# First attention stage of a two-block transformer kernel: order of DVE's work at two tiles of a head pair, the rotation's PSUM read, and three matmuls at the opening

## What is computed

```
qa = _rms(aq.reshape(B, N, ATT_KV_HEADS, ATT_GROUP, ATT_HEAD_DIM), att_q_norm).transpose(0, 2, 3, 1, 4)
ka = _rms(ak.reshape(B, N, ATT_KV_HEADS, ATT_HEAD_DIM), att_k_norm).transpose(0, 2, 1, 3)
q_lat = _rope(qa[:, :, :, n_ctx:], cos, sin)
k_all = jnp.concatenate([ka[:, :, :n_ctx], _rope(ka[:, :, n_ctx:], cos, sin)], axis=2)

s = jnp.einsum('bhgqd,bhkd->bhgqk', q, k, preferred_element_type=jnp.float32) * (ATT_HEAD_DIM ** -0.5)
p = jax.nn.softmax(s, axis=-1).astype(v.dtype)
return jnp.einsum('bhgqk,bhkd->bhgqd', p, v)
```

## Time and profile before

| what | value |
|---|---|
| median of 3 runs | 4217.92 us (4216.91 to 4218.13) |
| the profiled execution's own time | 4220.12 us |
| its span in the trace | 4218.3 us |
| PE busy | 3938.0 us (93%) |
| DVE busy | 1680.2 us (40%) |
| ACT busy | 851.4 us (20%) |
| POOL busy | 692.3 us (16%) |
| this phase, 308 to 498 us | 190 us |

### The profile page before, as it was taken

One profiled execution on the slowest core, in us unless ns is written; L12 is line 12 of the kernel. 1 busy time (PEld: TensorE's weight loads), 2 busy tenths in 40 slices (PEclk: granted clock), 3 DMA queues, 4 the chain that ended last, 5 costly groups with the idle time before them and its releaser, 6 DMA issues. The chain is left out here.

```text
span 4218.3 us, 51374 instructions
## 1 busy us (share of the span) xinstructions
PE 3938.0 (93%) x20867; PEld 2405.2 (57%) x20867; DVE 1680.2 (40%) x3134; ACT 851.4 (20%) x1663; POOL 692.3 (16%) x513
## 2 busy tenths in 40 slices
PE   7998889999999999899998999989998898999988
PEld 4565445554448666488745677768654444443333
DVE  2337343323764554533474656634124324111111
ACT  3224320000121333200013333321113201000000
POOL 0003212222420111123342332310002200000000
PEclk9999999999999999899998999999989998999999
DMA  5107611112541100254352010014200314999999
GB/s 175 40 11 285 198 40 60 60 60 95 170 126 56 46 31 26 93 217 160 111 173 50 26 31 26 19 39 154 63 0 1 155 46 192 406 420 422 422 421 374
DMA packets 323233, 580.12 MB, mean 138 GB/s; under 512 B 58700, under 2 KB 189228, under 8 KB 322360
## 3 DMA queue, kind: packets, MB, share of 16 engines
q1 hardware_dynamic: 323000, 576.83, 37.3%
HBM read 566.15 MB, written 10.63 MB: 137 GB/s over the span
## 5 line engine op out<-in xcount | busy, mean ns | idle before, releaser
L3348 PE MATMUL dn_ps<-room,dn_w 128*128 128x512 f32 (+1 forms) x616 | 230.2, 520 | 0.5 <-DVE dn_v_tok L3897 0.3
L961 PE MATMUL ffn_up_ps<-ffn_up_t,room 128*128 128x384 f32 (+1 forms) x704 | 208.3, 440 | 8.0 <-DVE room L1037 8.0
L961 PE MATMUL ffn_up_ps<-room 128*128 128x384 f32 (+1 forms) x704 | 203.9, 433 | 0.0
L4907 PE MATMUL experts_ps<-experts_ring,experts_xs 128*64 128x512 f32 (+1 forms) x768 | 164.1, 580 | 21.9 <-DMA experts_ring<-in_w_up 21.9
L961 PEld LDWEIGHTS ffn_up_ps<-ffn_up_t,room 128*128 128x128 f32 x704 | 136.0, 194 | 66.1 <-DVE room L1037 9.5
L1233 PE MATMUL ffn_down_ps<-ffn_down_w_sums,ffn_w 128*128 128x512 f32 x330 | 163.1, 604 | 10.8 <-DVE ffn_down_w_sums L1321 10.8
L2637 PE MATMUL hgrn_ps<-room,hgrn_w 128*128 128x512 f32 x372 | 170.3, 593 | 0.9 <-DVE hgrn_v L2891 0.9
L4907 PE MATMUL experts_ps<-experts_ring,room 128*64 128x512 f32 (+1 forms) x768 | 161.1, 570 | 8.7 <-DMA experts_ring<-in_w_up 8.1
L961 PEld LDWEIGHTS ffn_up_ps<-room 128*128 128x128 f32 x704 | 134.0, 190 | 55.5
L1044 DVE TENSOR_TENSOR room<-ffn_up_ps,room 128x384 f32<-128x384 f32 (+1 forms) x154 | 73.4, 489 | 222.2 <-PE ffn_up_ps L961 222.2
L5001 DVE TENSOR_TENSOR x_sb<-x_sb,experts_ps 128x512 f32<-128x512 f32 x56 | 38.5, 688 | 297.9 <-PE experts_ps L4842 297.9
(11 more groups left out here) (682 smaller groups left out, 7315.3 us busy)
## 6 DMA issues: line engine op xcount, KB each, us to landing
experts_ring<-in_w_gate SPq DMA_DIRECT2D x128, 704.0 KB, 14.9
experts_ring<-in_w_up SPq DMA_DIRECT2D x128, 704.0 KB, 16.7
experts_ring<-in_w_down SPq DMA_DIRECT2D x160, 512.0 KB, 13.7
att_wm<-in_mod_w SPq DMA_DIRECT2D x20, 2048.0 KB, 8.9
ffn_w<-in_ffn_w_down SPq DMA_DIRECT2D x37, 1024.0 KB, 4.9
ffn_up_wm<-in_ada_w SPq DMA_DIRECT2D x12, 2048.0 KB, 12.6
ffn_w<-in_ffn_w_up SPq DMA_DIRECT2D x22, 1024.0 KB, 7.6
ffn_front<-in_ffn_w_down SPq DMA_DIRECT2D x18, 1024.0 KB, 4.8
```

Source lines behind the costliest of these rows:

```text
L961: mm = nc.tensor.matmul(result(n, p), lhs[:, k, :], rhs[:, k, :], start=k == 0, stop=k == half - 1)
L3348: mm = nc.tensor.matmul(out, ahead.tile[:, k, :] if k < by_ahead else wt[:, h % 2, piece, k, :], hT[:, k, tok], start=k == 0, stop=k == KD ...
L4907: mm = nc.tensor.matmul(ps[out_rows, 3 * n + c, 0:b - a], xs_now[:, j, at:at + SLOTS], ring[:, w_at + a:w_at + b], start=j == 0, stop=j == ...
```

## The change

It has three parts, all in `even_attention`.

1. **First tile.** In pairs 2, 3 and 4 DVE runs the reciprocal and the normalising of unit `u` ahead of `highest(u + 1)`. At all other tiles the order is as before.
2. **Rotation.** `rope` is split. `rope_by_sin`, which reads bank 7, stands at the end of DVE's third tile, with its wait for `swapped`. `rope_by_cos` and the sum stay in the fourth tile. PE's `turn(u, 1)` of the fourth tile waits for the sine product alone (`rotated`), and the second wait for `roped`, ahead of the modulation, is gone.
3. **Opening.** Ahead of its first wait in the phase PE issues three float32 matmuls of 128x512 from the identity matrix into bank 6. Nobody reads their result.

```
+def keep_busy(nc, out, lhs, rhs, n):
+    for _ in range(n):
+        nc.tensor.matmul(out, lhs, rhs, start=True, stop=True)
...
+            keep_busy(nc, ps[:, 6, :].rearrange("p (a n) -> p a n", a=4), ident, ident.unsqueeze(1).broadcast_to([P, 4, P]), 3)
             pe.wait_ge(S["two_set"], 4)
...
                 if at == 3 and j + 1 < PAIRS:
-                    pe.wait_ge(S["roped"], j + 3)
+                    pe.wait_ge(S["rotated"], 2 * (j + 2) + 1)
...
-                if at == 3 and j + 1 < PAIRS:
-                    pe.wait_ge(S["roped"], j + 3)
...
-            def rope(i, bank, n):
+            def rope_by_sin(bank, n):
                 dve.wait_ge(S["swapped"], n)
                 if n > 1:
                     dve.wait_ge(S["roped"], n - 1)
+                nc.vector.tensor_tensor(tmp[:, 0, :], ps[:, bank, :], sin[:, :], ALU.mult).then_inc(S["rotated"], 1)
+
+            def rope_by_cos(i, n):
                 lat = raw[:, i, CTX:]
-                nc.vector.tensor_tensor(tmp[:, 0, :], ps[:, bank, :], sin[:, :], ALU.mult).then_inc(S["rotated"], 1)
                 nc.vector.tensor_tensor(tmp[:, 1, :], lat, cos[:, :], ALU.mult).then_inc(S["rotated"], 1)
                 dve.wait_ge(S["rotated"], 2 * n)
                 nc.vector.tensor_tensor(lat, tmp[:, 0, :], tmp[:, 1, :], ALU.add).then_inc(S["roped"], 1)
...
+            for u, (j, t) in enumerate(units):
+                at = u % TILES
+                after_context = at == 0 and j
+                if after_context:
+                    normed_b(u)
+                if u + 1 < len(units):
+                    highest(u + 1)
+                if not after_context:
+                    normed_b(u)
                 if u == 0:
                     modulated(len(OPENING_BANKS), OTHER)
                 if j + 1 < PAIRS and at == 3:
                     dve.wait_ge(S["gained"], j + 2)
-                    rope(j + 1, OTHER, j + 3)
+                    rope_by_cos(j + 1, j + 3)
                 if u < TILES:
                     read_out(u)
                 if at - 1 in mod_at(j):
                     modulated(OPENING + LOOP * j + mod_at(j).index(at - 1), OTHER)
                 if j + 1 < PAIRS and at == 1:
                     gained(j + 1)
+                if j + 1 < PAIRS and at == 2:
+                    rope_by_sin(OTHER, j + 3)
```

More of the change, by code:

```diff
@@ L2367, in _ @@
             dve.wait_ge(S["gained"], 1)
-            rope(0, 4, 1)
+            rope_by_sin(4, 1)
+            rope_by_cos(0, 1)
             dve.wait_ge(S["k_scaled"], 2)
-            rope(KEY, 5, 2)
+            rope_by_sin(5, 2)
+            rope_by_cos(KEY, 2)
             for m, bank in enumerate(OPENING_BANKS):
@@ L2392, in highest, with normed_b @@
                     nc.vector.scalar_tensor_tensor(s[:, 1, a:a + 1], s[:, 0, a:a + 1], -1.0, rs[:, j, t, a:a + 1], ALU.mult, ALU.mult).then_inc(S["max_done"], 1)
-            highest(0)
-            for u, (j, t) in enumerate(units):
+            def normed_b(u):
+                j, t = units[u]
                 s = st[:, u % 2, :, :]
-                at = u % TILES
-                if u + 1 < len(units):
-                    highest(u + 1)
                 dve.wait_ge(S["exp_done"], 2 * u + 2)
@@ L2406, in _ @@
                 nc.vector.tensor_scalar(flat, flat, s[:, 3, 1:2], None, ALU.mult).then_inc(S["b_normed"], 1)
+            highest(0)
+            for u, (j, t) in enumerate(units):
[7 more added lines that the diff above has]
+                    normed_b(u)
                 if u == 0:
```

## The result

The changed kernel takes 4232.9 us in the median of 6 runs (4227.95 to 4236.88), the kernel before 4218.02 us (6 runs, 4215.26 to 4218.85). The ratio is 1.0036, with a 95% interval of 1.0023 to 1.0049: 15 us slower. The forecast was 6.7 us slower and its range ended at 4231.0. So the sign of the sum was right, its size was not.

A forecast was written before the change was run, and what follows sets the result against it. The prediction took PE, nearly always busy but with 35 us idle between its pieces, as the bound. First tiles -4.0, rotation waits +9.0, clock +2.2 and opening -0.5 gave +6.7 us, so 4224.6 us, range 4218.5 to 4231.0.

The forecast's parts named there:

- The term of 9.0 us for the waits: At three rotations, PE's second transposes start 3.0 us later each, behind DVE's late normalising and POOL's 3.15 us call.
- The first tiles: First tiles of pairs 2 to 4: earlier normalising gains 1.8, 1.8 and 0.4 us, 4.0 us in all.
- the clock term: PE's longer idle time at the rotations makes half clock likely: 2.2 us lost, between 0 and 4.6.
- The price of one spell: Half clock behind a rotation costs 0.8 us on the second transposes and up to 1.1 us on the modulation.
- The discount of half for cover: Much of the half-clock cost at a rotation lies over waits, so 1.1 us was taken, a little more than half.
- already pays for one: Pair 1's rotation has half clock in the kernel before, so the clock loss counts twice 1.1 us, not three times.
- The opening: Three matmuls ahead of PE's stream at the phase's start: 0.5 us gained, bounded by DVE's 0.60 us of idle time.
- The spreading half clock: Rival, chance 0.28: half clock covers transposes and modulation at all three rotations; +11.2 us, 4229.1 us.
- The rule of the Trainium skill: By it POOL would keep 2.63 us and block DVE's cosine product; the prediction held that the trace disagrees.
- POOL at 2.63 us: Rival, chance 0.14: POOL's call at the rotations is not stretched and the clock holds; +3.0 us, 4220.9 us.
- the late stream: Rival, chance 0.04: PE's opening stream ends late at half clock, 1.8 us lost; +9.0 us, 4226.9 us.
- the swap lands in time: Rival, chance 0.04: the swap precedes DVE's arrival, so each rotation saves PE's 1.19 us; -8.1 us, 4209.8 us.

The follow-up runs named there:

- second trace: The changed kernel run and traced again with no edit; 4231.2 us, ratio 1.003 to the kernel before.
- split alone: The changed kernel without the opening matmuls and with the first tiles in their old order, leaving only the rotation's split; 4235.23 us, ratio 1.0038 to the kernel before.
- part 3 alone: The kernel before plus only the three opening matmuls; 4219.87 us, ratio 1.0006.
- cosine early: The changed kernel with DVE's cosine product moved ahead of the swap in the third tile and the sum moved to the fifth tile; 4226.99 us, one run.

## Why the prediction failed, by its own steps

**What came as written.** At each rotation PE waits 2.58 us on DVE (2.7 predicted) and 1.30, 1.30 and 0.92 on POOL (1.4), DVE idles 2.61 us ahead of the sine product (2.6), and POOL takes 3.15. The term of 9.0 us for the waits measures 3 x 2.94 = 8.8. The first tiles in pairs 2 and 3 gave 1.8 and 2.1 us against 1.8 each, pair 4's 0.45 (456.01 to 462.57 before, 470.74 to 476.85 now) against 0.4: 4.3 against 4.0. For pairs 2 and 3 that agreement is partly luck. The forecast had 1.3 us for the new order and 0.5 for the clock, but of the gain about 1.3 and 1.6 us are half clock that went away with the 2.07 us gap; what the new order buys at full clock is pair 4's 0.45. The start at 384.60 from which the 1.3 us were counted was itself late by half clock: the scores ahead of it took 2.41 us, 1.56 at full clock.

**The step that failed is the size of the clock term.** The forecast said: a spell costs up to 0.8 us on the second transposes and up to 1.1 on the modulation, "much of it will lie over waits, so I take 1.1 us". The pieces above 22.65 us are 3.65, 2.55 and 3.46 in the changed kernel, 2.27, 3.36 and 2.36 in its second trace, and 2.61, 2.75 and 2.82 with the split alone: 2.9 us on average in nine rotations, and none without. Before paid 1.5 in pair 1 (21.23 - 19.71). The term is therefore 9.7 - 1.5 = 8.1 us in the profiled execution (2.1, 2.5 and 3.5 us in pairs 1 to 3, where 0, 1.1 and 1.1 stood), 6.5 in the second, where 2.2 stood and 4.6 was the upper bound. Two things were wrong in it:

- The price of one spell. I took the modulation from rows 10, 3.00 us, but that was one which the clock left on its way; one wholly at half clock takes 3.60, 1.67 above 1.93. And the spell reaches further than the two rows that I priced. Pair 1 shows it:

```profile
365.20 1.97 PE L2200 MATMUL att_ps<-cst,att_probs 128*128 128x128 f32 x8 [1.30 <-POOL att_probs L2324]
367.89 1.09 PE L2223 MATMUL att_ps<-cst,room 128*128 128x128 f32 x4 [0.72 <-ACT att_pT L2304]
...
372.43 1.12 PE L2200 MATMUL att_ps<-cst,att_probs 128*128 128x128 f32 x4
373.48 1.81 PE L2168 MATMUL att_ps<-even_raw 64*128 64x256 f32 x8
```

  Against the same rows at full clock (1.09, 0.63, 0.66 and 1.56 us) these are 0.88 + 0.46 + 0.46 + 0.25 us, with the modulation's 1.67 in all 3.72. The piece was 3.65 us longer.
- The discount of half for cover. 3.72 by the rows and 3.65 by the piece means that, from the second transposes on, next to nothing was covered; in pairs 2 and 3 the same sums give 2.61 and 3.52 us by the rows and 2.55 and 3.46 by the piece. The wait behind the second transposes, on ACT's copy, was 0.72 us and 0.77 before, so it hid 0.05. Only what is slowed ahead of the wait on POOL is covered: in pair 3 the scores took 1.08 us in place of 0.70, and that wait was 0.92 us in place of 1.30. Neither of the two rows that I priced stands there.

Pair 1 "already pays for one" was right in kind and too much in size: what it paid, 1.5 us, was less than half of what it pays now, since the spell then began only at the transposes of the scan (1.08 us in place of 0.63), behind the second transposes, and ended within the modulation.

**The opening**, -0.5 us in the sum, came to +0.24 us in the profiled execution and -0.10 in the second trace, and part 3 alone to no gain. Of DVE's 0.60 us of idle time nothing was left in the first trace and 0.31 in the second. But in the first trace DVE's scaling ahead of its squares, which waits for a transfer, began 8.67 us behind the phase's start and not 7.90, and the piece varies by more than that from run to run (49.13 to 51.52 us in eleven of twelve traces).

**Not in the sum**: the last piece gained 1.35 us more than the first tile in it. It is a spell that the kernel before had in pair 4 and the changed kernel in this trace had not. PE of the kernel before, behind a wait without a releaser in the row, and then the modulation of the changed kernel at the same place:

```profile
480.67 2.55 PE L2125 MATMUL att_ps<-att_wm,conditions 128*2 128x128 f32 x64 [2.83 <-issue]
483.15 1.12 PE L2193 MATMUL att_ps<-cst,att_probs 128*128 128x128 f32 x4
484.59 5.67 PE L2210 MATMUL att_ps<-att_pT,even_av 128*64 128x512 f32 x24 [0.33 <-DVE att_mod L2328]
...
494.48 1.93 PE L2131 MATMUL att_ps<-att_wm,conditions 128*2 128x128 f32 x64 [1.58 <-ACT att_pT L2304]
```

The changed kernel's three rows take 1.93, 0.66 and 5.37 us, 1.38 less, while PE's waits from pair 4's first modulation to the next stage add up to the same in both traces (11.56 and 11.60 us). In the second trace such a spell came again, at pair 4's modulation before this one (3.34 us). So these 1.3 us are no gain of the change. And 1.4 and 3.8 us of the profiled execution are from outside the phase. The phases of the two traces are 11.5 and 10.0 us longer, the medians 14.9 and 12.5; where the other 3.4 and 2.5 us come from stays open. The range is missed only with them: 4217.92 + 11.5 = 4229.4 us lies within it. The failed step stands apart from that, since the clock term alone is 5.9 us off.

With the term at its measured size the sum is -4.3 + 8.8 + 8.1 + 0.2 - 1.3 = 11.5, the difference of the phase.

**The rivals.** The spreading half clock was the right mechanism and the nearest number (4229.1), but it too had 1.9 us for a spell, and expected the gain at the first tiles to shrink. There the clock held in all traces with part 1. POOL at 2.63 us and the late stream did not come. That the swap lands in time was rightly held unlikely: DVE reached the wait 2.61 us early. The upper end of the range, 4231.0, was built on 4.6 us as the most that the clock could take, which is three spells at 1.9 us each less the 1.1 that pair 1 was taken to pay already.

**The rule of the Trainium skill.** The prediction set the Trainium skill's rule ("SBUF — State Buffer", section "SBUF: two separate sides", an exclusive lock held for the whole instruction) against the trace. The runs bear the trace out: DVE's cosine product ran its 0.68 us inside POOL's call, and POOL's call grew by 0.52 us, in the changed kernel and, at the short call, beside the sum. Nobody was blocked to the end of the other's instruction: the sum behind the cosine product, slowed to 1.19 us, ended at 407.79, POOL's call at 408.55.

## What to carry to other kernels

Before you move a step ahead of a wait, look at when the engine gets there: DVE came to the swap 2.6 us early, and what had filled that time was the very work that PE needs next; relaxing PE's wait in place, with nothing moved, took 0.75 us of the 1.19 at two of three rotations and cost nothing. A gap on PE has two prices, its own length and what the clock takes from the work behind it, and the second lengthens the path wherever no later wait of PE gets shorter by it: price it row by row up to where the clock returns, from a row wholly at half clock, and without a discount for cover unless you can name the wait that covers it. Where a wait can't be avoided, matmuls that nobody reads in front of it held the clock here at all three rotations and gave back 5.7 us in the median, of the 8.0 that the spells took in the trace beside it.

## What the runs showed of the hardware

- **How the spells follow the gaps.** With gaps of 2.58 and 0.3 to 1.3 us at a rotation, 12 of 12 rotations (four traces) ran into half clock. With one of 1.19 us, 4 of 12 (four traces) did. With 0.40 us none of 9, and with filled gaps (0.86 and 0.24 us left) none of 3. At the first tiles the gap of 2.07 us brought a spell 6 times of 6 in pairs 2 and 3, but only once of 3 in pair 4 (none in before); the gap of 1.65 never did, in 21 first tiles of seven traces. In pair 4 a wait of 2.2 to 3.0 us ahead of a late modulation was followed by a spell in 5 of 9 traces (2.28, 2.51, 2.64, 2.83 and 3.03 us) and not in 4 (2.23, 2.30, 2.43 and 2.53). So a gap's length alone doesn't decide. What else does is open; each kernel has one trace, the changed one two.
- **A spell's price.** It was 1.5 to 1.6 us where it began behind a gap of 1.19 us, and 2.3 to 3.7 us behind the pair of gaps of the changed kernel and of the split alone. In "cosine early", with POOL's call shorter in pairs 2 and 3, it was 2.9, 2.3 and 0.8 us (above 22.65 us, and in those two above 22.13, POOL being 0.52 us shorter); in pair 3 the clock was back behind the second transposes.
- **POOL beside DVE.** A product or sum of two SBUF operands (0.68 us) that DVE starts early in POOL's multiplication lengthens that by 0.52 us: from 2.63 to 3.15 us for 128x768 where it starts 0.5 us behind POOL (38 calls in the twelve traces, no exception), and from 1.08 to 1.60 for 128x256 where it starts 0.2 us behind (26 calls). In 33 calls of 128x768 it started 1.7 to 2.2 us behind POOL, and the call took 2.62 or 2.63. Why the late ones cost nothing is open. A second one behind an early one in the same call, 1.2 us behind POOL's start, did not lengthen POOL further (3.15 with the cosine product and the sum), but took 1.19 us itself. Why the second is slowed and not POOL was not tried.
- **Time outside the edit.** The unchanged stages behind the phase took 3.8 us longer in one trace of the changed kernel and 0.5 in the other, and 3715.5 to 3721.6 us over all twelve traces, so differences of 2 us in the whole can't be read from single runs. But the pieces with a rotation or a first tile repeat to 0.02 us from kernel to kernel wherever the order is the same and the clock is full.
